# A 5-layer fp32 transformer on one core: heads' squares summed as two fp32r products, and changed orders at six places

## The chip, the cores and the metric

One core of a Trainium2 chip. The metric is the device time of one execution in microseconds (us); smaller is better. The kernel takes 1498.96 us, the median of three runs (1498.57 to 1501.03). All of the kernel is one hand-written program for the five engines: TensorE (PE, with its weight loads as PEld), VectorE (DVE), ScalarE (ACT), GpSimd (POOL) and SyncE (SP, which only issues transfers).

## The reference

For 256 positions of width 1024, in float32, four layers of one block and then one layer of another:

```python
for layer in range(4):                       # mixers: diff, stick-breaking, sliding window, diff
    h = rmsnorm(x, attn_norm[layer]); m = mixer(h)
    x = x + m @ w_o[layer]
    h = rmsnorm(x, ffn_norm[layer]); x = x + conv_gated_ffn(h)      # 2752 wide, causal conv of 3
x = rmsnorm(x, final_norm)
h = rms_norm(x, g_mix_pre); y = concat(pool_mixer, moba_attention)(h) @ w_out
x = x + rms_norm(y, g_mix_post)
h = rms_norm(x, g_ffn_pre); x = x + rms_norm(conv_ffn(h), g_ffn_post)
x = x + (p @ w_ple) * sigmoid(x @ w_ple_gate)
```

In the differential mixer (layers 0 and 3) each of the 8 heads has an output `o` of 128 columns per position, which is normalised by itself: `rmsnorm(o, subln) * (1 - lambda_init)`. That needs the sum of the squares over the head's 128 columns.

## The kernel before

**Numbers.** Everything is float32. A product runs as three fp32r matmuls: every operand is split into a high part (a cast to fp32r) and a low part (the rest), and hi x hi, lo x hi and hi x lo are summed in PSUM. A plain fp32 matmul is recorded as two matmuls of one line (the "x2" of the rows). Plain fp32 is used for the small things: scores, transposes, probabilities x values, and sums over partitions by a matmul with a matrix of ones (statistics).

**Weights.** They come as 245 chunks of 128x2048, in the order in which TensorE uses them. SP fetches a chunk into one of three raw buffers; ACT writes its high part `w_hi` (L394); DVE writes its low part `w_lo` (L919, raw minus high); TensorE uses both. SP's fetch of the third chunk after it waits for DVE's low part, which frees the raw buffer. How far ahead of use a chunk is split is written out by hand: `ahead(c, lead)` and `split_to(c)` stand at chosen places of ACT's and DVE's programs.

**Order.** Each engine's program is one fixed queue over the list STAGES (mixer projections and heads, `wo`, `up`, `down`, per layer); semaphores join them. An instruction that waits holds up everything behind it on its engine.

**Normalisation.** TensorE starts a stage before the row statistic is known: the first chunk or chunks (`raw_chunks`) use x times the gain ("raw" tiles `h_hi`, `h_lo`), and their outputs are scaled afterwards (`scaled_first`, and L1444 for `up`). Behind them `normalise` (DVE) writes hf, ACT casts it to `h_hi` (`split_h`, L444), DVE writes the even low tiles (L961) and POOL the odd ones (`low_odd`, L1544). The statistic itself is a matmul in the middle of the first chunk (`statistic`, called in `first_outputs`).

**Differential heads.** Heads go in pairs, 4 groups per layer, 16 heads in the two layers. For a head TensorE multiplies probabilities by values (`heads`, L1916 and L1917). ACT copies the result (`head_squares`, L483) and squares it (L485). TensorE sums the squares over the partitions (`head_statistic`, L1968: plain fp32 ones x squares). ACT takes the logarithm and the exponential (`head_rms`, L490 and L493), DVE scales the head (L1078), ACT and DVE split it (L499, L1083), and it is an operand of `wo`. Between these TensorE runs other work (`beside`): the projections of the next group, or, in the last group, the first parts of `wo`. An even head's statistic stands ahead of the transposes of the next head (L1905), and behind them in the last group; an odd head's stands after the next scores or next to the last `wo` parts. DVE splits chunks between its other duties (`ahead`), one of them right after the divide of the odd head, which is where the even head's squares are made. POOL, in these layers, issues the bias tables' transfers (`bias_dma`, L1539, two for each head, in a loop) and nothing else after the layer's first low tiles.

**Other places the change touches.** Layer 0's start (`first_layer`); the last group of the stick-breaking heads (`mask` on POOL, L1626, between ACT's exponential and TensorE's `heads`); the eight sliding-window head pairs (`copy_probT` L472, `exps` L464, `mix_high` L478 on ACT; `divide`, `mix_low` L1072 on DVE; TensorE's `heads` wait for both); the first two chunks of `up` and the fifth, which waits for its low part; the start of layer 4 (`mix`), where the statistic of `down3` stands after the third tile; the residual and second normalisation of layer 4 (`add_normed` L1058, L1067); and the last `add_normed` ahead of the gate.

## Time and profile before

| what | value |
|---|---|
| median of the runs | 1498.96 us (1498.57 to 1501.03) |
| the profiled execution's own time | 1498.88 us |
| its span, first to last instruction | 1497.2 us |
| granted TensorE clock, mean | 0.999 of full speed |
| busy: PE / PEld | 1487.0 us (99%) / 1423.4 us (95%) |
| busy: DVE / ACT / POOL | 1063.5 us (71%) / 879.2 us (59%) / 336.2 us (22%) |
| from memory | 262 MB, 176 GB/s over the span |
| chain that ended last, by engine | PE 87%, DVE 8%, ACT 3%, issue 1% |

The table is to be read so: where TensorE is busy nearly all the time, an instruction taken from it shortens the run by its place in the queue, and idle time of another engine is worth nothing in itself. What can be won otherwise is the few short stretches in which TensorE waits, and what can be lost is a new one.

### The profile page before, as it was taken

The numbers are of one execution on the slowest core, as the hardware profiler recorded it, in microseconds if no ns is written. First come the engines' busy times: TensorE is split into PE (matmuls) and PEld (weight loads), VectorE is DVE, ScalarE is ACT, GpSimd is POOL, SyncE is SP. The second block draws the span as 40 slices with busy tenths as digits, with TensorE's granted clock in tenths as the row PEclk, the third lists the DMA queues.
The fourth block names the chain that finished last, engine by engine and source line by source line (L and its number), as shares of the span: only waits on it lengthen the run. The fifth ranks groups of instructions, "written<-read, shape, count | busy, mean of one in ns | idle before, by whom it ended". The sixth has DMA issues, their size and how long they took to land.

```text
span 1497.2 us, 28533 instructions
## 1 busy us (share of the span) xinstructions
PE 1487.0 (99%) x11576; PEld 1423.4 (95%) x11576; DVE 1063.5 (71%) x1734; ACT 879.2 (59%) x1405; POOL 336.2 (22%) x482
## 2 busy tenths in 40 slices
PE   9999999999999999999999999999999999999998
PEld 8999999899999998989999899999998899999998
DVE  7778877565578775786887566688775778776545
ACT  7777655456766554575656347766563567544343
POOL 2103222211142222213222221032222371221101
PEclk9999999999999999999999999999999999999999
DMA  7643656443336554552665545446554554365450
GB/s 272 204 162 124 242 184 218 169 163 147 117 138 218 205 190 177 187 180 85 216 207 183 188 170 178 155 145 221 197 192 177 173 191 169 114 228 194 164 209 29
DMA packets 39694, 265.16 MB, mean 177 GB/s; under 512 B 5247, under 2 KB 5562, under 8 KB 8976
## 3 DMA queue, kind: packets, MB, share of 16 engines
q1 hardware_dynamic: 36432, 255.54, 48.4%
q0 software_dynamic: 2992, 7.79, 2.3%
q8 instruction: 91, 1.49, 0.4%
q14 instruction: 35, 0.29, 0.1%
q10 hardware_dynamic: 144, 0.05, 0.0%
HBM read 262.24 MB, written 1.12 MB: 176 GB/s over the span
## 4 chain that ended last, share of the span: by engine, by line
PE 87%; DVE 8%; ACT 3%; issue 1%; POOL 0%; ACTq 0%
PE bank L1681 21%; PE bank L1682 20%; PE bank L1683 20%; PE bank L1692 9%; PE bank L1691 4%; PE bank L1733 4%; DVE w_lo L919 4%; PE bank L1742 2%; ACT w_hi L394 1%; PE bank L1916 1%; DVE tmp L1454 1%; PE bank L1897 1%; PE bank L1896 1%; DVE tmp L965 1%; PE bank L1905 1%
## 5 line engine op out<-in xcount | busy, mean ns | idle before, releaser
L919 DVE TENSOR_TENSOR w_lo<-w_raw,w_hi 128x2048 fp32r<-128x2048 f32 x239 | 553.0, 2321 | 72.5 <-ACT w_hi L394 72.3
L1681 PE MATMUL bank<-h_hi,w_hi 128*128 128x256 f32 x1968 | 561.2, 285 | 0.8 <-DVE w_lo L919 0.8
L1682 PE MATMUL bank<-h_lo,w_hi 128*128 128x256 f32 x1968 | 556.8, 283 | 0.0
L1683 PE MATMUL bank<-h_hi,w_lo 128*128 128x256 f32 x1968 | 556.8, 283 | 0.0
L394 ACT CAST w_hi<-w_raw 128x2048 fp32r<-128x2048 f32 x239 | 453.0, 1905 | 85.3 <-DMA w_raw<-w_std 64.4
L1681 PEld LDWEIGHTS bank<-h_hi,w_hi 128*128 128x128 f32 x1968 | 377.3, 192 | 6.4 <-issue 4.2
L1682 PEld LDWEIGHTS bank<-h_lo,w_hi 128*128 128x128 f32 x1968 | 377.4, 192 | 0.1
L1683 PEld LDWEIGHTS bank<-h_hi,w_lo 128*128 128x128 f32 x1968 | 377.3, 192 | 0.0
L1692 PE MATMUL bank<-act_both,w_hi 128*128 128x512 f32 x672 | 239.0, 399 | 0.0
L1454 DVE SCALAR_TENSOR_TENSOR tmp<-bank,par,tmp 128x255 f32<-128x255 f32 (+1 forms) x346 | 149.1, 476 | 94.6 <-ACT tmp L854 93.5
L1691 PE MATMUL bank<-act_both,w_lo 128*128 128x256 f32 x672 | 188.9, 281 | 0.0
L854 ACT ACTIVATE tmp<-bank,par 128x256 f32<-128x256 f32 x173 | 88.8, 558 | 157.0 <-PE bank L1683 156.9
L1692 PEld LDWEIGHTS bank<-act_both,w_hi 128*128 128x128 f32 x672 | 126.4, 188 | 30.0
L1652 POOL CAST act_both<-tmp 128x256 f32 x110 | 53.7, 488 | 440.2 <-DVE tmp L1471 336.5
L1681 PE MATMUL bank<-act_both,w_hi 128*128 128x256 f32 x516 | 149.2, 289 | 0.0
L1682 PE MATMUL bank<-act_both,w_hi 128*128 128x256 f32 x516 | 145.9, 283 | 0.0
L1683 PE MATMUL bank<-act_both,w_lo 128*128 128x256 f32 x516 | 145.9, 283 | 0.0
L1691 PEld LDWEIGHTS bank<-act_both,w_lo 128*128 128x128 f32 x672 | 127.0, 189 | 0.0
L1733 PE MATMUL bank<-h_hi,w_hi 128*128 128x256 f32 x384 | 102.5, 289 | 0.0
L1681 PEld LDWEIGHTS bank<-act_both,w_hi 128*128 128x128 f32 x516 | 98.7, 191 | 3.0 <-issue 2.7
L1733 PE MATMUL bank<-h_hi,w_lo 128*128 128x256 f32 x384 | 100.3, 283 | 0.0
L1682 PEld LDWEIGHTS bank<-act_both,w_hi 128*128 128x128 f32 x516 | 98.8, 191 | 0.1
(219 smaller groups left out, 2116.2 us busy)
## 6 DMA issues: line engine op xcount, KB each, us to landing
w_raw<-w_std SPq DMA_DIRECT2D x239, 1024.0 KB, 4.8
act_both<-vec_dram POOLq DMA_DIRECT2D x56, 128.0 KB, 3.4
w_raw<-w_std SPq DMA_DIRECT2D x3, 512.0 KB, 7.8
x<-xT SPq DMA_DIRECT2D x2, 512.0 KB, 5.2
out<-x SPq DMA_DIRECT2D x3, 256.0 KB, 2.0
w_raw<-w_std SPq DMA_DIRECT2D x2, 256.0 KB, 4.8
par<-params SPq DMA_DIRECT2D x1, 446.0 KB, 6.0
cst<-consts SPq DMA_DIRECT2D x1, 256.0 KB, 8.8
```

The lines of the kernel that those rows point to most:

```text
L394: act.copy(w_hi[:, n % SLOTS, :], w_raw[:, n % RAW, :]).then_inc(hi_ready, 1)
L854: act.activation(to[:, slot, :], source, ACT.Identity, bias=col(3), scale=col(2)).then_inc(conv_init, 1)
L919: dve.tensor_tensor(w_lo[:, n % SLOTS, :], w_raw[:, n % RAW, :], w_hi[:, n % SLOTS, :].bitcast(F32), ALU.subtract).then_inc(lo_ready, 1)
L1454: return dve.scalar_tensor_tensor(to[:, slot, lag:S], source(v)[:, 0:S - lag], par[:, bass.ds(at + (4 * v + 2 - lag), 1)], to[:, slot, lag:S],
L1652: pool.tensor_copy(act_hi[:, bass.ds(j, 1), :].squeeze(1) if not isinstance(j, int) else act_hi[rows, j, :], cval[rows, slot, :]).then_inc ...
L1681: pe.matmul(dst, wh, xh, start=first, stop=False, skip_group_check=shared)
L1682: pe.matmul(dst, wh, xl, start=False, stop=False, skip_group_check=shared)
L1683: done = pe.matmul(dst, wl, xh, start=False, stop=last, skip_group_check=shared)
L1691: pe.matmul(bank[:, 0:S], wl, xh, start=start and k == 0, stop=False, skip_group_check=True)
L1692: done = pe.matmul(bank[:, :], wh, pair, start=False, stop=stop and k == len(weights) - 1, skip_group_check=True)
L1733: pe.matmul(dst, a, b, start=k == 0 and w is wh and (n == 0 or not shared), stop=False, skip_group_check=shared)
L1742: done = pe.matmul(dst, a, b, start=False, stop=k == DT - 1, skip_group_check=shared)
```

## The change

The squares of a head get a high and a low part. ACT casts the squares to fp32r (`square_hi`), POOL subtracts (`square_lo`, two operands from SBUF), and TensorE sums each with an fp32r matrix of ones, which ACT makes once per differential layer in the buffer of `tri_r`. The even head's statistic goes behind the transposes in all groups. The rest are changed orders: an earlier split of chunk 2 in layer 0; a later second split in the last stick-breaking group; ACT's and DVE's order in the sliding-window heads; the split of `up` chunk 5 ahead of the second chunk's taps, with a shorter wait on TensorE; in layer 4 a second raw chunk, and the statistic of `down3` after the sixth tile; and, for the two `add_normed`, gains multiplied by ACT while it takes the outputs, all low tiles of the second normalisation on DVE, each right behind the next tile.

The parts below stand in the order of the program: the buffers and ACT's lead in the last group, ACT (`head_squares`, the mixer stages, the sliding window, `wo` and `down` of layer 4), DVE (`normalise`, `add_normed`, the first layer, the start of `mix`, the last stick-breaking group, the sliding window, `up`), POOL (`square_low_of`, `low_odd`), and PE (`statistic`, the start of `mix`, the heads, `up`).

```diff
+        ones_r = tri_r
+        square_hi, square_lo = act_hi[:, DT + 2:DT + 4, :], act_lo[:, DT + 2:DT + 4, :]
...
-            return 3 if app == 0 else 2 if app % 2 and app < 9 else 1
+            return 3 if app == 0 else 2 if app % 2 and app < 9 or app == 8 else 1
...
                 act.activation(u_sb[:, 2 + slot, :], u_sb[:, slot, :], ACT.Square).then_inc(head_sq, 1)
+                act.wait_ge(head_sq, d_half + 1)
+                act.copy(square_hi[:, slot, :], u_sb[:, 2 + slot, :]).then_inc(square_high, 1)
...
+                    if c0 == 0:
+                        split_to(2)
                     (both_rms if prev == "down3" else rms)(SUMS[prev][2])
...
-                            if k:
-                                act.wait_ge(bank_free, RING + c0 + 1)
-                                act.wait_ge(used, c0 + k + 1)
-                                act.copy(u_sb[:, 2 * k:2 * k + 2, :].rearrange("p a b -> p (a b)"),
-                                         pj[slot_of(c0, k)][:, :]).then_inc(bank_free, 1)
                             ahead(c0 + k)
+                        act.wait_ge(bank_free, RING + c0 + 2)
...
+                        if da:
+                            act.wait_ge(consts_in, 16)
+                            act.copy(ones_r[:, :], ones).then_inc(ones_high, 1)
...
                             q, s = half + j, s_half + j
-                            copy_probT(s, j % 2, 2)
+                            if j not in (2, 6):
+                                copy_probT(s, j % 2, 2)
                             if j == 5:
                                 ahead(c0 + 6, HIGH)
+                                mix_high(q, j)
+                                copy_probT(s + 1, 0, 2)
                             if j < 6:
                                 exps(s + 2, j % 2, j + 3)
+                            if j != 5:
+                                mix_high(q, j)
                             if j in (1, 3):
                                 evac_q(c0 + 4 + j // 2, j // 2)
-                            mix_high(q, j)
+                            if j == 1:
+                                copy_probT(s + 1, 0, 2)
...
-                        done = act.copy(tmp[:, a:b, :].rearrange("p a b -> p (a b)"), source)
+                        for t in range(a, b):
+                            done = act.mul(tmp[:, t, :], source[:, (t - a) * S:(t - a + 1) * S], param("mix_post", t))
...
+                    if every:
+                        if k:
+                            low(k - 1)
...
-                    dve.scalar_tensor_tensor(tmp[:, k, :], tmp[:, k, :], param(gain, k),
-                                             factor, ALU.mult, ALU.mult).then_inc(dve_step, 1)
+                    dve.tensor_tensor(tmp[:, k, :], tmp[:, k, :], factor, ALU.mult).then_inc(dve_step, 1)
...
+                split_to(2)
                 dve.wait_ge(rstd_done, 1)
                 scaled(0, 1, 2, 3)
-                split_to(2)
...
+                        if kind == "mix":
+                            scaled_first(c0 + 1, u_sb[:, 2:4, :], (1.0, 1.0))
...
+                            mix_low(q, i * 2)
+                            if not more:
                                 ahead(c0 + n, HIGH)
-                            mix_low(q, i * 2)
...
+                            mix_low(half + j, j)
                             if j < 6:
                                 steps[0] += divide(s_half + j + 2, j % 2, True, steps[0])
-                            mix_low(half + j, j)
...
-                                if j == 0:
-                                    split_to(weights_of(layer, c) + RING)
+                                split_to(weights_of(layer, c) + RING)
...
+            def square_low_of(d_half, slot):
+
+                pool.wait_ge(square_high, d_half + 1)
+                pool.tensor_tensor(square_lo[:, slot, :], u_sb[:, 2 + slot, :],
+                                   square_hi[:, slot, :].bitcast(F32), ALU.subtract).then_inc(square_low, 1)
...
                         with pool.Fori(1, halves // 2) as i:
                             for b in range(2):
                                 bias_dma(table, i * 2 + (s_half + b), b, i * 2 + b)
+                            for b in range(2):
+                                square_low_of(i * 2 + (d_half - 2 + b), b)
+                        for b in range(2):
+                            square_low_of(d_half + halves - 2 + b, b)
...
-                    for k in range(lead):
-                        project(c0 + k, slot_of(c0, k), app, prev if k == 0 else None)
+                    if lead:
+                        project(c0, slot_of(c0, 0), app, prev, False)
+                        project(c0 + 1, slot_of(c0, 1), app, "raw")
...
+                    if da:
+                        pe.wait_ge(ones_high, layer // 3 + 1)
...
-                        pe.wait_ge(head_sq, d + 1)
-                        pe.matmul(tp[1][:, 0:S], ones, u_sb[:, 2 + slot, :], start=True, stop=True)\
+                        pe.wait_ge(square_low, d + 1)
+                        pe.matmul(tp[1][:, 0:S], ones_r[:, :], square_hi[:, slot, :], start=True, stop=False)
+                        pe.matmul(tp[1][:, 0:S], ones_r[:, :], square_lo[:, slot, :], start=False, stop=True)\
                           .then_inc(head_stat, 1)
...
-                        if da and more:
-                            head_statistic(d, 0)
                         transposes(s + 1, 1, maps)
-                        if da and not more:
+                        if da:
                             head_statistic(d, 0)
...
-                        if k == RING and layer < 4:
+                        if k in (RING, RING + 1) and layer < 4:
                             pe.wait_ge(lo_ready, weights_of(layer, c) + 1)
-                            pe.wait_ge(first_scaled, first_scaled_count(ffn, 1))
+                            pe.wait_ge(first_scaled, first_scaled_count(ffn, 2 * (k - RING) + 1))
```

## Rows read from the trace of the kernel before

**Rows 1.** The page: busy us of each engine, share of the span, instructions.

```profile
PE 1487.0 (99%) x11576; PEld 1423.4 (95%) x11576; DVE 1063.5 (71%) x1734; ACT 879.2 (59%) x1405; POOL 336.2 (22%) x482
```

**Rows 2.** Waits of PE: engine, what waits, for what: us, times, longest.

```profile
PE bank L1842 <- DVE acc L953: 1.1, 1, 1.1
PE bank L1681 <- DVE w_lo L919: 1.0, 5, 0.2
PE bank L1916 <- DVE act_both L1072: 0.9, 2, 0.5
PE bank L1742 <- DVE h_lo L961: 0.7, 2, 0.4
PE bank L1916 <- issue: 0.5, 1, 0.5
PE bank L1742 <- POOL h_lo L1544: 0.5, 1, 0.5
PE bank L1916 <- ACT tmp L472: 0.5, 3, 0.2
```

**Rows 3.** Timeline of PE at `up`: start us, us, what, xcount [idle before].

```profile
148.04 0.28 PE L1683 MATMUL bank<-h_hi,w_lo 128*128 128x256 f32 x1
148.55 0.39 PE L1681 MATMUL bank<-h_hi,w_hi 128*128 128x256 f32 x1 [0.22 <-DVE w_lo L919]
148.77 0.28 PE L1682 MATMUL bank<-h_lo,w_hi 128*128 128x256 f32 x1
148.89 0.29 PE L1683 MATMUL bank<-h_hi,w_lo 128*128 128x256 f32 x1
```

**Rows 4.** Timeline of PE, layer 0: a statistic, the last group's heads and statistic.

```profile
88.82 0.59 PE L1968 MATMUL bank<-u_sb,cst 128*128 128x256 f32 x2
89.25 0.49 PE L1905 MATMUL bank<-cst,tmp 128*128 128x128 f32 x3
...
89.70 0.28 PE L1682 MATMUL bank<-w_lo,h_hi 128*128 128x256 f32 x1
...
108.44 0.70 PE L1916 MATMUL bank<-tmp,vtok 128*128 128x256 f32 x2 [0.15 <-ACT tmp L472]
...
111.34 0.59 PE L1968 MATMUL bank<-u_sb,cst 128*128 128x256 f32 x2
```

**Rows 5.** Single lines: count, shortest/median/longest ns, first to last start us.

```profile
L1968 PE MATMUL bank<-u_sb,cst x32: 377/379/382, 44.5 to 979.7; 128*128 128x256 f32 x32
...
L444 ACT CAST h_hi<-tmp x80: 391/407/410, 28.6 to 1281.6; 128x256 fp32r<-128x256 f32 x80
...
L1559 POOL TENSOR_TENSOR h_lo<-proj,h_hi x39: 730/740/876, 121.7 to 1262.0; 128x256 fp32r<-128x256 f32 x39
```

**Rows 6.** Timeline of ACT, layer 0: squares (L485) and a logarithm (L490).

```profile
86.54 0.42 ACT L485 ACTIVATE u_sb<-u_sb 128x256 f32<-128x256 f32 x1
...
105.80 0.42 ACT L485 ACTIVATE u_sb<-u_sb 128x256 f32<-128x256 f32 x1
...
108.32 0.48 ACT L490 ACTIVATE u_sb<-bank,odd 128x256 f32<-128x256 f32 x1
...
110.51 0.42 ACT L485 ACTIVATE u_sb<-u_sb 128x256 f32<-128x256 f32 x1
```

**Rows 7.** Timeline of POOL in layer 0's `up`.

```profile
138.53 2.79 POOL L1544 TENSOR_TENSOR h_lo<-tmp,h_hi 128x256 fp32r<-128x256 f32 x1
```

**Rows 8.** Timeline of DVE: the low parts of five weight chunks.

```profile
43.10 2.28 DVE L919 TENSOR_TENSOR w_lo<-w_raw,w_hi 128x2048 fp32r<-128x2048 f32 x1
...
86.62 2.29 DVE L919 TENSOR_TENSOR w_lo<-w_raw,w_hi 128x2048 fp32r<-128x2048 f32 x1
...
106.60 2.28 DVE L919 TENSOR_TENSOR w_lo<-w_raw,w_hi 128x2048 fp32r<-128x2048 f32 x1
...
110.58 2.28 DVE L919 TENSOR_TENSOR w_lo<-w_raw,w_hi 128x2048 fp32r<-128x2048 f32 x1
...
137.85 2.86 DVE L919 TENSOR_TENSOR w_lo<-w_raw,w_hi 128x2048 fp32r<-128x2048 f32 x1
```

More of the change, by code:

```diff
@@ L225, in build @@
         head_sq = sem("head_sq")
+        ones_high = sem("ones_high")
+        square_high = sem("square_high")
+        square_low = sem("square_low")
         head_stat = sem("head_stat")
@@ L880, in _ @@
                             squares(name, k, pj[slot_of(c0, k)][:, 0:S])
-                            act.copy(tmp[:, k, :], pj[slot_of(c0, k)][:, 0:S]).then_inc(bank_free, 1)
+                            act.mul(tmp[:, k, :], pj[slot_of(c0, k)][:, 0:S], param("ffn_post", k))\
+                               .then_inc(bank_free, 1)
                             if k == 2:
@@ L953, in add_squares, with normalise @@
                         dve.tensor_tensor(total, a, b, ALU.add).then_inc(acc_done, 1)
-            def normalise(app, norm, behind=None):
+            def normalise(app, norm, behind=None, every=False):
                 dve.wait_ge(rstd_done, norm + 1)
@@ L966, in normalise @@
                                              ALU.mult, ALU.mult).then_inc(hf_done, 1)
-                    if k % 2 and k > 1 and behind is None:
+                    if every:
+                        if k:
+                            low(k - 1)
+                    elif k % 2 and k > 1 and behind is None:
                         low(k - 3)
+                if every:
+                    low(DT - 1)
+                    return
                 if behind is not None:
@@ L1053, in divide, with add_normed @@
                 return done
-            def add_normed(gain, factor, signal, after):
+            def add_normed(factor, signal, after):
                 def scaled(k):
-                    dve.scalar_tensor_tensor(tmp[:, k, :], tmp[:, k, :], param(gain, k),
-                                             factor, ALU.mult, ALU.mult).then_inc(dve_step, 1)
+                    dve.tensor_tensor(tmp[:, k, :], tmp[:, k, :], factor, ALU.mult).then_inc(dve_step, 1)
                     steps[0] += 1
@@ L1395, in _ @@
                         dve.wait_ge(rstd_done, SUMS[name][2] + 1)
-                        add_normed("mix_post", mix_rstd, x_ready, sum_behind)
+                        add_normed(mix_rstd, x_ready, sum_behind)
                         ahead(c0 + 2, AHEAD)
-                        normalise(app, SUMS["res_a"][2])
+                        normalise(app, SUMS["res_a"][2], every=True)
                         ahead(c0 + 1, AHEAD)
@@ L1510, in low @@
                                                   ALU.subtract).then_inc(h_lo_even, 1)
-                        add_normed("ffn_post", rstd[:, :], hf_done, low)
+                        add_normed(rstd[:, :], hf_done, low)
                         split_to(CHUNKS)
@@ L1639, in _ @@
                     raw_low(app)
-                    low_odd(app, hf)
+                    if layer < 4:
+                        low_odd(app, hf)
                     app += 1
@@ L1750, in first_outputs @@
                             statistic("x")
-                    elif raw not in (None, "x", "raw") and k == {"d": 2, "w": 4}.get(raw[0], 5):
+                    elif raw not in (None, "x", "raw") and k == (5 if raw == "down3" else {"d": 2, "w": 4}.get(raw[0], 5)):
                         statistic(raw)
```

13 lines of the change are left out of this document (7 added, 6 removed).

## The prediction

> **What bounds the kernel.** I read the page's busy times first: PE is busy for 1487.0 us, 99% of its span, DVE for 71%, ACT for 59%, POOL for 22% [rows 1]. So only two things count: what PE itself executes, and the short stretches in which it waits. The second view is the list of PE's waits; the change aims at seven of its lines, which hold 5.2 us of idle time together [rows 2]. The third is PE's timeline around one such wait: at 148.04 the last product of a chunk starts, the next at 148.55 after 0.22 us of idle time and the one after at 148.77. That is 0.73 us for what takes 0.24 in a row without a break (two steps of 0.12, as from 148.77 to 148.89) [rows 3]. So a wait ahead of an fp32r product costs its idle time and about 0.27 us of emptying and refilling on top. Then come PE's rows at two statistics of the heads [rows 4], the single lines' durations [rows 5], and what ACT, POOL and DVE do at the same moments [rows 6 to 8], since the new subtraction runs on POOL while DVE splits weights.
>
> The terms are summed against the profiled execution's own time, 1498.88 us, with its span of 1497.2 in it; the median of the runs is 0.08 us above that, so the two are the same here. A measurement of this kernel can tell about 0.2% from no change, 3.0 us: "same" is 1496.0 to 1502.0.
>
> **Part 1, the heads' statistics, on PE.** The plain statistic takes from 88.82 to 89.25 [rows 4], 0.43 us; two fp32r products take 2 x 0.12 = 0.24 [rows 3]. Saved: 0.19 us for each of 16 heads, 3.0 us if nothing waits.
>
> **Part 1, the new chain.** Behind the squares stands a cast on ACT (0.41 us by L444, same shape [rows 5], 0.44 with its start), then a subtraction on POOL, both inputs from SBUF. Its nearest undisturbed row is L1559, 0.74 us [rows 5]. But one of its inputs there comes from PSUM. With both from SBUF, one that started at 138.53, inside DVE's low part of a chunk (137.85 to 140.71), took 2.79 us and ended at 141.32, 0.61 behind it [rows 7, 8]. DVE's low part has two SBUF inputs too and takes 2.28 us [rows 8]. So I bound a subtraction by 0.74 us on one side and "end of the low part plus 0.61" on the other, and take the second wherever a low part covers its start, since that row has its operands.
>
> The Trainium skill ("SBUF — State Buffer", section "SBUF: two separate sides") says that VectorE with two SBUF inputs and a GpSimd operation that reads SBUF exclude each other for the whole instruction. By that rule alone the subtraction would take its full 0.74 us behind the low part instead of 0.61: ten stalls x 0.13, which would make the sum 1501.3 instead of 1500.0.
>
> *Ordinary even heads (5).* The squares start at 86.54 [rows 6]; the cast ends near 87.4, inside the low part of 86.62 to 88.91 [rows 8]. The subtraction is ready at 88.91 + 0.61 = 89.52. PE arrives behind the transposes, 89.25 to 89.70 with a pipeline that overlaps by 0.12 [rows 4]: 88.82 + 0.33 = 89.15. Stall 0.37, less 0.19 saved: +0.18 each, +0.9 in all.
> *First even head.* Low part from 43.10, statistic at 44.5 [rows 5, 8]: ready at 45.38 + 0.61 = 45.99, arrival 44.83, stall 1.1: +0.9.
> *Ordinary odd heads (6).* No low part lies over their chain and they have over 1 us to spare: -0.19 each, -1.1.
> *Even head of the last group (2).* Squares end at 106.22 [rows 6], the cast at 106.66, just inside the low part of 106.60 to 108.88 [rows 8]. Ready at 109.49, the sums end at 109.73, and the next head's product starts at 109.83 instead of 108.44 [rows 4]: +1.4 each, +2.8.
> *Odd head of the last group (2).* The even head's late statistic moves its logarithm from 108.32 [rows 6] to about 110.0, and with DVE's scaling behind that the next low part from 110.58 to 112.28 [rows 8]. It ends at 114.56. The squares, at 110.51 [rows 6], come 1.4 later, so their cast ends at 112.8, inside it; ready at 115.17. PE arrives at 111.34 [rows 4] + 1.4 = 112.74: stall 2.43, with 0.1 of restart and 0.19 saved +2.35 each, +4.7.
> Part 1 together: 0.9 + 0.9 - 1.1 + 2.8 + 4.7 = **+8.2 us**.
>
> **Part 1, what it puts beside other work.** ACT gets 16 casts and two copies of the ones, under 8 us on an engine that is 59% busy [rows 1]; where its copy for the next head is already what PE waits for (0.15 us [rows 4]), a cast of 0.44 ahead of it could show, but there the subtraction is later still and hides it. With that gone it would cost up to 0.44 a group. POOL's two bias transfers of a group now stand behind its subtractions, so they go out up to 3 us later; the table is wanted a group later (the even heads of two neighbouring groups lie 20 us apart, 88.82 and 108.44 [rows 4]). No other queue is passed.
>
> **Part 2, the six changed orders.** *`up`, the fifth chunk's low part:* PE waits for it 5 times, 1.0 us, 4 in `up`, one at the start [rows 2]; with 0.27 of restart each 2.3 us. It goes because the low part now stands ahead of the second chunk's taps. Late next are these taps, by up to 1.8 us; PE no longer waits for both of them at once, only for the chunk's own, and POOL's split behind may be held by the low part as above. Between 0 and 2.3 gained, or worse (a rival). I take 2.3. SP's fetch behind each low part moves with it, by at most 4 us, against buffers two chunks ahead.
> *The start of layer 0:* chunk 2's low part 3 us earlier, with the transfer behind it; small stalls, 0.15 us, and at worst one new wait of the same size.
> *Layer 4's start:* the statistic of `down3` waits 1.1 us for DVE's sum (L1842) [rows 2]; three tiles later and with a second raw chunk, it goes with its restart: 1.3. ACT's and DVE's scaling of the second raw chunk adds 0.7 us of DVE, beside PE's next chunk.
> *Second normalisation:* PE waits twice for DVE's low tiles (L961), 0.7 [rows 2]. POOL's low tiles go, and so does what they hold back; each tile is then a product and a low part on DVE. 0.7 + 0.54 = 1.25, at worst 0, if DVE's pace per tile is just PE's.
> *The last `add_normed`:* 0.5 <- POOL h_lo [rows 2] with 0.27, of which I take half, 0.4.
> *Last stick-breaking group:* 0.5 before L1916, which the list calls issue [rows 2]; 0.55.
> *Sliding window:* 0.9 <- act_both and the part of 0.5 <- ACT tmp that isn't the two last groups' 0.15 [rows 2, 4], 0.2: 1.1.
> Sum: 2.3 + 0.15 + 1.3 + 1.25 + 0.4 + 0.55 + 1.1 = **-7.1 us**. For layer 4's `wo`, where multiplications take the place of copies on ACT, I add nothing: they hide beside the raw chunks' products on PE; without that cover they would cost up to 0.75 us.
>
> **Net:** +8.2 - 7.1 = +1.1. 1498.9 + 1.1 = **1500.0 us**, no change that can be measured. Its own range, with each bound of part 2 and 0.3 us either way on the last group's four stalls, is 1497 to 1503.
>
> **Rivals.**
> *A. POOL is not held.* L1559's 0.74 us speak for it [rows 5], the row at 138.53 against it [rows 7]. Then every ordinary head gains 0.19, 12 x 0.19 = 2.3; the last even heads lose some 0.4 by ACT's cast ahead of the copy; the last odd ones, squares ended at 110.93 [rows 6], are ready at 110.93 + 0.44 (shift) + 0.44 + 0.15 + 0.74 = 112.7 against 111.8: +0.8 each. Part 1 is +0.1, the time 1498.9 - 7.1 + 0.1 = 1491.9 us. Chance 0.15.
> *B. The wait at `up` comes back one chunk later.* The taps stand behind a low part of 2.28 us, or 2.86 where POOL is in its way [rows 8], and the chunk after next waits for its own. I put their slack at 0.7 to 0.9 us, an estimate. It decides where they come more than that late: then the 1.8 gained in the four `up` is gone and 4 x 1.3 of new wait (0.9 to 1.0 of lateness, 0.27 restart) comes: 1500.0 + 1.8 + 5.2 less what overlaps, 1504.5 us, slower. For it speaks that DVE's split and POOL's exclude each other [rows 7]; against it that the wait now is only 0.2 us long at its longest [rows 2]. Chance 0.12.
> *C. It doesn't do what it says:* the restarts don't come back with the idle time, and part 2 brings 5.2 of idle at most, or half of it, 2.6 to 5.2: 1502 to 1504 us. Chance 0.05.
> The main case has 0.68.
>
> **How the numbers follow.** The predicted time is the main case's, 1500.0. Its range of 1497 to 1503 holds about 0.8 of its 0.68; to leave out no more than 2 in 10 in all, the range goes down towards A, to 1493, and up to B's 1504.5. Faster by over 0.2%: all of A, 0.15, and 0.06 of the main case. Slower: all of B, most of C, and 0.14 of the main case, where its two largest terms, the last groups' stalls, run over: 0.30. Same: the rest, 0.49.
>
> **What would show it right or wrong.** In the changed profile PE's waits should list the statistic's line <- POOL square_lo: some 10 entries, about 0.37 us five times, 1.1 once, and the longest in the last groups, 1 to 2.4 us. Each of the late subtractions should last 1 to 2.5 us and end 0.6 behind a w_lo; if they all last 0.74, A is right. L1842, w_lo, act_both, h_lo and L1916's issue should be gone from the waits. A new wait of `up` on u_sb or act would show B. If PE's busy time doesn't fall by about 3 us, the two products don't take 0.24. The forecast fails if the subtraction's wait sits in another place than the last groups, or if what frees PE there is not POOL but ACT.

## The result, and the profile after

The changed kernel takes 1515.4 us (median; 1514.97 to 1515.95, 4 runs) where the kernel before took 1499.06 in the same session: a ratio of 1.0108, 95% interval 1.0096 to 1.012. That is 16.3 us slower, where 1500.0 was forecast with a range of 1493 to 1504.5. The profiled execution spans 1514.1 us, 16.9 more than before.

The page of the changed kernel, busy us of each engine (beside [rows 1]):

```profile
PE 1489.3 (98%) x11576; PEld 1426.6 (94%) x11576; DVE 1063.6 (70%) x1740; ACT 887.5 (59%) x1425; POOL 373.8 (25%) x494
```

and TensorE's waits in it (what waits, for what: us, times, longest; beside [rows 2]):

```profile
PE bank L2006 <- POOL act_both L1603: 9.7, 10, 2.4
PE bank L1716 <- ACT tri_r L602: 3.7, 1, 3.7
PE bank L1931 <- DVE small L1023: 2.2, 1, 2.2
PE bank L1777 <- POOL h_lo L1567: 1.9, 1, 1.9
PE bank L1716 <- ACT vtok L519: 1.5, 1, 1.5
...
PE bank L1931 <- ACT proj L738: 0.6, 1, 0.6
PE bank L1951 <- DVE act_both L1093: 0.2, 1, 0.2
```

Five of the seven old lines are gone, as forecast (L1842 <- acc, w_lo, DVE's h_lo, the issue entry, ACT's L472), act_both has shrunk to 0.2, and the statistic (now L2006) waits for POOL's subtraction (L1603) ten times. But four lines are new and a fifth has grown, none of them forecast: for the ones in fp32r (L602), for scores and token copies in layer 4 (L1023, L519), for POOL's low tile in the last stage (L1567, 1.9 where it was 0.5), and for ACT's copy in the sliding window (L738).

PE's busy time rose by 2.3 us where a fall of about 3 was to show that two products take 0.24. They do: where nothing waits, the statistic's two products and the next one start 0.12 apart (96.25, 96.36 and 96.48 us in e9). Busy time also grows where the clock is low, which four of these waits brought with them (below): in e4, with the same products and one such stretch, it is 1484.3.

How far the changed kernel's TensorE lies behind the one before at the same product tells where the time went. The steps of that distance (us, + is later) are these:

| place | forecast | measured |
|---|---|---|
| layer 0, up to 27 us | -0.6 | -1.1 |
| layer 0, wait for the ones | 0 | +5.2 |
| statistics, 12 ordinary heads | +0.7 | +0.8 |
| last groups, even heads (2) | +2.8 | +2.7 |
| last groups, odd heads (2) | +4.7 | +6.3 |
| `up`, 4 times | -1.8 | -1.8 |
| last stick-breaking group | -0.55 | -0.6 |
| sliding window | -1.1 | -0.6 |
| statistic of `down3` | -1.3 | -1.4 |
| layer 4's heads | 0 | +5.5 |
| second normalisation | -1.25 | -1.0 |
| last stage | -0.4 | +2.85 |
| sum | +1.1 | +16.9 |

Three rows hold 14 of the 15.8 us by which the forecast was short, and two of them were forecast as nothing.

**The ones.** TensorE in the changed kernel, layer 0, then ACT (start us, us, what [idle before]):

```profile
29.62 0.28 PE L1718 MATMUL bank<-w_hi,h_lo 128*128 128x256 f32 x1
33.62 0.58 PE L1716 MATMUL bank<-h_hi,w_hi 128*128 128x256 f32 x1 [3.72 <-ACT tri_r L602]
34.00 0.41 PE L1717 MATMUL bank<-h_lo,w_hi 128*128 128x256 f32 x1
34.21 0.41 PE L1718 MATMUL bank<-h_hi,w_lo 128*128 128x256 f32 x1
```

```profile
33.03 0.21 ACT L587 ACTIVATE root_gain<-root_gain 128x8 f32<-128x8 f32 x1
33.27 0.30 ACT L602 CAST tri_r<-cst 128x128 fp32r<-128x128 f32 x1
```

The copy of the ones costs ACT 0.30 us, but it stands in ACT's queue behind the first head's exponentials, which wait for scores, and TensorE waits for it ahead of the first group of heads, although the ones are first used at 49.4 us. The trace of the kernel before showed it: there the instruction ahead of the new copy ends at 34.3 us, and TensorE passes the place of the new wait at 30.8.

```profile
34.11 0.21 ACT L578 ACTIVATE root_gain<-root_gain 128x8 f32<-128x8 f32 x1
```

**The heads.** POOL's subtractions and DVE's low parts of chunks in the changed kernel, layer 0 (beside [rows 7, 8]):

```profile
91.90 2.02 POOL L1603 TENSOR_TENSOR act_both<-u_sb,act_both 128x256 fp32r<-128x256 f32 x1 [5.26 <-ACT act_both L492]
99.70 0.75 POOL L1603 TENSOR_TENSOR act_both<-u_sb,act_both 128x256 fp32r<-128x256 f32 x1 [5.78 <-ACT act_both L492]
111.30 2.74 POOL L1603 TENSOR_TENSOR act_both<-u_sb,act_both 128x256 fp32r<-128x256 f32 x1 [10.85 <-ACT act_both L492]
117.75 2.01 POOL L1603 TENSOR_TENSOR act_both<-u_sb,act_both 128x256 fp32r<-128x256 f32 x1 [3.71 <-ACT act_both L492]
```

```profile
91.04 2.29 DVE L935 TENSOR_TENSOR w_lo<-w_raw,w_hi 128x2048 fp32r<-128x2048 f32 x1
...
111.17 2.29 DVE L935 TENSOR_TENSOR w_lo<-w_raw,w_hi 128x2048 fp32r<-128x2048 f32 x1
116.89 2.29 DVE L935 TENSOR_TENSOR w_lo<-w_raw,w_hi 128x2048 fp32r<-128x2048 f32 x1
```

The subtraction outside a low part takes 0.75 us; the three inside one end 0.58 to 0.59 behind it (91.90 + 2.02 = 93.92 against 93.33; 114.04 against 113.46; 119.76 against 119.18). The forecast had 0.61.

The row of the 12 ordinary heads agrees with its forecast partly by luck. The first even head was to stall for 1.1 us and cost 0.9; TensorE came late to it, behind the wait for the ones, and it cost 0.33. The other five even heads cost 0.32 each instead of 0.18: the idle time was shorter than forecast (0.25 at 93.98 us, for 0.37), but the emptying and refilling behind it, about 0.27 us, had been left out of their sum. The six odd ones gained 0.18 each, as forecast.

**The clock.** The same stall cost 2.5 us in layer 0 and 3.8 in layer 3. Here are two products behind it in each, and the windows over them (length; busy us and count of PE, PEld, DVE, ACT and POOL; the last three numbers are the granted clock, the share of the DMA engines and GB/s). The third window lies behind the wait for POOL's low tile in the last stage:

```profile
119.81 0.39 PE L2006 MATMUL bank<-act_both,tri_r 128*128 128x256 f32 x1 [2.41 <-POOL act_both L1603]
120.03 0.28 PE L2007 MATMUL bank<-act_both,tri_r 128*128 128x256 f32 x1
...
989.69 0.58 PE L2006 MATMUL bank<-act_both,tri_r 128*128 128x256 f32 x1 [2.42 <-POOL act_both L1603]
990.07 0.41 PE L2007 MATMUL bank<-act_both,tri_r 128*128 128x256 f32 x1
```

```profile
120.00:121.50 1.50, 1.50 (x14) 1.50 (x14) 0.19 (x1) 0.89 (x2) 0.00 (x0) 1.00 0.89 191
...
990.00:992.60 2.60, 2.60 (x13) 2.60 (x13) 0.65 (x2) 1.30 (x3) 0.00 (x0) 0.50 0.99 312
...
1487.00:1491.50 4.50, 4.50 (x26) 4.50 (x27) 3.09 (x3) 4.48 (x3) 2.12 (x3) 0.62 0.00 0
```

After 2.41 us of idling the granted clock stayed at 1.00 in one place; after 2.42 us it was 0.50 (the lower level, 1.2 GHz) for 2.6 us in the other, twelve products came every 0.213 us instead of 0.12, and that cost 12 x 0.093 = 1.1 us more. Behind the wait for the ones it was thirteen products, 1.2 us: 3.72 us of idle time, 0.42 of emptying and refilling and this 1.2 come to 5.35, and 0.2 of it the kernel before loses at the same products too, which leaves 5.2. In the last stage fifteen products came so, 1.4 us, and in layer 4 ten. The Trainium skill ("TensorE: Matmul & The Clock Gate", Part 1) says that a gate sets TensorE's clock by how busy it has been recently, and that the number of products at the lower clock varies from run to run. The traces agree: each stretch at 0.50 here follows a wait of 1.5 to 3.7 us, and behind the same wait of 3.72 us for the ones it was 13 products in this run and 21 in e5.

**Layer 4.** DVE at the scores of the second head pair, and some of POOL's pooling windows ahead of it, in the changed kernel:

```profile
1244.68 0.06 DVE L1016 MEMSET wait_mark<- 128x1 f32 x1 [6.97 <-DMA act_both<-vec_dram]
```

```profile
1204.78 2.26 POOL L1633 TENSOR_TENSOR sq<-sq,par 128x16 f32<-128x16 f32 x1
1207.01 2.84 POOL L1634 TENSOR_SCALAR sq<-sq 128x240 f32<-128x240 f32 x1
...
1214.50 2.14 POOL L1633 TENSOR_TENSOR sq<-sq,par 128x16 f32<-128x16 f32 x1
1216.61 2.84 POOL L1634 TENSOR_SCALAR sq<-sq 128x240 f32<-128x240 f32 x1
...
1239.88 2.21 POOL L1562 DMA_DIRECT2D act_both<-vec_dram  x4 [0.30 <-POOL act_both L1638]
```

The same transfers in the kernel before:

```profile
1224.04 2.20 POOL L1539 DMA_DIRECT2D act_both<-vec_dram  x4 [0.30 <-POOL act_both L1609]
```

The pooling windows are a chain of small operations on POOL from 1203.94 to 1239.6, 35.6 us; before it ran from 1193.51 to 1223.7, 30.2 us. L1633 takes 0.22 us when nothing is in the way and 2.14 to 2.35 where it meets a low part. Seven operations of the chain last over 2 us so, four did before. Behind the chain stand the transfers of the next table. In the kernel before they left at 1224.04; TensorE is 9.6 us later here, so they leave 6.3 us later against its work (5.4 by the chain, 0.9 by its start); DVE waits 7 us for them, and TensorE waits for DVE's scores (2.2) and ACT's copies behind these (1.5).

**The last stage.** POOL's first low tile, and DVE meanwhile, in the changed kernel:

```profile
1482.10 4.75 POOL L1567 TENSOR_TENSOR h_lo<-x,h_hi 128x256 fp32r<-128x256 f32 x1 [60.25 <-ACT h_hi L909]
```

```profile
1482.15 0.42 DVE L1088 TENSOR_TENSOR x<-x,tmp 128x256 f32<-128x256 f32 x1
1482.49 0.42 DVE L1080 TENSOR_TENSOR tmp<-tmp,rstd 128x256 f32<-128x256 f32 x1
...
1485.51 0.75 DVE L1088 TENSOR_TENSOR x<-x,tmp 128x256 f32<-128x256 f32 x2
```

POOL was held through twelve DVE operations in a row and ended 0.59 behind the last of them (1486.85 against 1486.26), where DVE paused for the first time. Of the 2.85 us, 1.4 are the longer wait (1.9 for 0.5) and 1.4 the lower clock behind it. In the kernel before the same tile took 1.14 us, and the DVE operation that it met 0.96 instead of 0.48. There DVE's scaling was a scalar_tensor_tensor that read its gain from SBUF (`par`):

```profile
1468.22 1.14 POOL L1544 TENSOR_TENSOR h_lo<-x,h_hi 128x256 fp32r<-128x256 f32 x1 [60.43 <-ACT h_hi L893]
```

```profile
1468.68 0.96 DVE L1058 SCALAR_TENSOR_TENSOR tmp<-tmp,par,rstd 128x256 f32<-128x256 f32 x1
```

### The profile page after: what moved, and what is told of

It reads as the page before. It is cut to its first block, busy times and chain, and to the rows that moved or that the text cites. A ratio compares the mean times of both kernels' runs of the same rounds, so it can differ in the third digit from the quotient of the medians.

```text
span 1514.1 us, 28578 instructions
## 1 busy us (share of the span) xinstructions
PE 1489.3 (98%) x11576; PEld 1426.6 (94%) x11576; DVE 1063.6 (70%) x1740; ACT 887.5 (59%) x1425; POOL 373.8 (25%) x494
## 4 chain that ended last, share of the span: by engine, by line
PE 87%; POOL 4%; DVE 3%; ACT 3%; issue 2%; DMA 0%; POOLq 0%; ACTq 0%; DVEq 0%
PE bank L1716 19%; PE bank L1717 19%; PE bank L1718 19%; PE bank L1727 10%; PE bank L1768 6%; PE bank L1726 5%; PE bank L1777 3%; POOL act_both L1603 1%; ACT tmp L469 1%; PE bank L1951 1%; DVE tmp L1023 1%; PE bank L2301 0%; POOL sq L1634 0%; POOL sq L1633 0%; DVE w_lo L935 0%
```

## The experiments

The kernel before was timed in each session beside them: 1499.35 us with e1 to e4, 1498.75 with e5 to e8, 1499.39 with e9 to e11. Unless an edit says otherwise, it is made on the changed kernel.

**e1: the heads' part undone.**

```diff
-                act.copy(square_hi[:, slot, :], u_sb[:, 2 + slot, :]).then_inc(square_high, 1)
...
-                        pe.wait_ge(square_low, d + 1)
-                        pe.matmul(tp[1][:, 0:S], ones_r[:, :], square_hi[:, slot, :], start=True, stop=False)
-                        pe.matmul(tp[1][:, 0:S], ones_r[:, :], square_lo[:, slot, :], start=False, stop=True)\
+                        pe.wait_ge(head_sq, d + 1)
+                        pe.matmul(tp[1][:, 0:S], ones, u_sb[:, 2 + slot, :], start=True, stop=True)\
```

> The changed kernel with the heads' part undone (plain fp32 sum of the squares, no cast, no subtraction, no ones in fp32r, even statistic back ahead of the transposes), the six changed orders kept. My theory: the heads' part costs 5.3 us by TensorE's wait for the ones in layer 0, 3.8 and 5.1 us in the two last groups and 0.8 us in the ordinary groups, 15.0 us together, so about 1500.4 us. Rival, by the forecast on record: the heads' part costs 8.2 us, so 1507.2 us, and the six orders cost the rest. Second rival: the waits only stand for others that take their place, and less than 5 us come back, above 1510 us.

Measured: 1501.45 us (1500.8 to 1506.09, 10 runs), ratio 1.0018, interval 1.0008 to 1.0028. The heads' part costs 13.9 us, not 8.2, and the six orders together, forecast at 7.1 us faster, make the kernel 2 us slower. The profiled execution was one of the longer ones (1505.2): DVE waited 2.5 us in layer 0 for the first bias transfer, and TensorE 2.5 for DVE. Without that wait and what comes with it (3.9 us) the two profiled executions are 14.4 us apart.

**e2: the wait for the ones ahead of the first statistic.**

```diff
-                    if da:
-                        pe.wait_ge(ones_high, layer // 3 + 1)
...
+                        pe.wait_ge(ones_high, layer // 3 + 1)
                         pe.wait_ge(square_low, d + 1)
```

> The changed kernel with one edit: TensorE waits for the fp32r ones only ahead of the first statistic, not ahead of the first group of heads. My theory: the 3.7 us wait at 29.6 us goes with its restart and the lower granted clock behind it, 5.3 us in all, so 1510.1 us, and nothing takes its place. Rival: ACT's queue is late there for its other work too, and the next product that needs ACT (its token copies, or the split of the next chunk) waits in its stead: at least 1513.5 us.

Measured: 1511.52 us, ratio 1.0084 (1.0067 to 1.0101). The 3.7 us wait is gone and no other stands in its place; at 37 us TensorE is 5.2 us ahead of the changed kernel. 0.8 of that is given back at the first even head, whose subtraction TensorE now reaches early enough to wait for, 1.09 us where the forecast had 1.1:

```profile
45.18 0.36 PE L2005 MATMUL bank<-act_both,tri_r 128*128 128x256 f32 x1 [1.09 <-POOL act_both L1603]
```

The wait for the ones had hidden that stall.

**e3 and e5: how DVE multiplies in the last stage.**

```diff
-                    dve.tensor_tensor(tmp[:, k, :], tmp[:, k, :], factor, ALU.mult).then_inc(dve_step, 1)
+                    dve.scalar_tensor_tensor(tmp[:, k, :], tmp[:, k, :], 1.0,
+                                             factor, ALU.mult, ALU.mult).then_inc(dve_step, 1)
```

> The changed kernel with one edit: in the two add_normed DVE multiplies by a scalar_tensor_tensor with the number 1.0 in place of a tensor_tensor (same operands, same result). My theory: POOL's first low tile of the last stage, which took 4.75 us, is held by an unbroken row of tensor_tensor operations and gets its turn where a scalar_tensor_tensor stands in the row, as in the kernel before; it lasts about 1.1 us again and the wait of 1.9 us for it shrinks to 0.5 or less: 1512.3 to 1513.0 us. Rival: only the tightness of DVE's row counts (no pause between its operations), not the kind of operation, and nothing changes: 1515.4 us, the POOL operation above 4 us again.

Measured: 1517.43 us (1514.94 to 1520.07), ratio 1.012 (1.01 to 1.014). The POOL operation lasts 4.75 us again: my theory fell as I had put it, since the kind of operation alone changes nothing. Its profiled execution (1517.8) is 2.1 us longer than the changed kernel's for another reason: DVE waited 1.9 us for the first bias transfer in layer 0, and TensorE 5.8 instead of 3.7 for the ones. In e5 the 1.0 is `ones[:, 0:1]`, a column in SBUF.

> The changed kernel with one edit: in the two add_normed DVE multiplies by a scalar_tensor_tensor whose scalar is read from a column of ones in SBUF (as the kernel before read its gain), where the run with the number 1.0 in the instruction left POOL's 4.75 us as it was. Theory: what lets POOL in is that DVE must read this scalar from SBUF before it takes its two tiles; POOL's first low tile of the last stage lasts about 1.1 us again, the wait for it falls from 1.9 to at most 0.5 us, and the last stage is 2.5 to 2.9 us shorter. Rival: POOL got in before only because ACT was later or DVE's row had a pause somewhere; then the POOL operation lasts above 4 us again.

Measured: 1514.47 us (2 runs), ratio 1.0092 (1.0062 to 1.0123), and, what tells, POOL and DVE in e5:

```profile
1483.81 1.14 POOL L1568 TENSOR_TENSOR h_lo<-x,h_hi 128x256 fp32r<-128x256 f32 x1 [60.43 <-ACT h_hi L909]
```

```profile
1483.93 0.42 DVE L1089 TENSOR_TENSOR x<-x,tmp 128x256 f32<-128x256 f32 x1
1484.26 0.96 DVE L1080 SCALAR_TENSOR_TENSOR tmp<-tmp,cst,rstd 128x256 f32<-128x256 f32 x1
```

1.14 instead of 4.75 us, and now it is DVE's operation that is held (0.96 instead of 0.48): POOL took its turn just where DVE had a scalar to read from SBUF. TensorE's wait for that tile is gone, and the last stage is 3.0 us shorter than the changed kernel's. The whole run gained only 0.9 us, in two runs, and 1.5 in the profiled execution. There 21 and 14 products behind two earlier waits came at the lower clock, where the changed kernel's profile has 13 and 12 behind its two, and five more in layer 4: 1.4 us.

**e4: the transfers ahead of the fourth pooling window.**

```diff
                         for g, w in enumerate(WINDOWS):
+                            if g == 3:
+                                for h in range(2, halves):
+                                    bias_dma(table, s_half + h, h % 2, h)
```

> The changed kernel with one edit: in layer 4 POOL issues the bias transfers of the second head pair ahead of the fourth pooling window, not behind it. My theory: DVE's wait of 7.0 us for that transfer, and with it TensorE's waits of 2.2 and 1.5 us and the low clock behind them, go: 5.5 us less, 1509.9 us. Rival: the fourth window, now 2.2 us later, is what TensorE waits for instead (its product for the pooled tiles stands at 1242.95 us, and POOL ended at 1239.6): a new wait of up to 1.5 us, 1511 to 1512 us. Second rival: the stall belongs to the second raw chunk itself and not to the transfer: no change, 1515.4 us.

Measured: 1512.24 us, ratio 1.0089 (1.0072 to 1.0106). Of TensorE's waits in e4 this one is new:

```profile
PE bank L1719 <- POOL act_both L1641: 1.5, 1, 1.5
```

The waits for scores and token copies are gone, and over layer 4's heads TensorE gains 3.7 us on the changed kernel: the transfer was the cause. The first rival is right about the rest: the fourth window now ends 4.6 us later, 2.1 by the four issues ahead of it and the rest because three of its operations now last 2.1 to 2.7 us, where two lasted 2.2 and 2.4.

**e10: the start of layer 4 put back.** One raw chunk, the statistic behind the third tile, ACT copying the second chunk's outputs.

```diff
-                    elif raw not in (None, "x", "raw") and k == (5 if raw == "down3" else {"d": 2, "w": 4}.get(raw[0], 5)):
+                    elif raw not in (None, "x", "raw") and k == {"d": 2, "w": 4}.get(raw[0], 5):
...
-                        project(c0 + 1, slot_of(c0, 1), app, "raw")
...
-                            scaled_first(c0 + 1, u_sb[:, 2:4, :], (1.0, 1.0))
```

> The changed kernel with the start of layer 4 put back as before: one raw chunk, the statistic behind the third tile, ACT copying the second chunk's outputs. Theory: the 5.5 us lost behind the late transfer come from this edit alone (POOL's windows start later against DVE's chunk splits and are held more often); it goes, and the gain of 1.3 us at the statistic is lost: 1515.4 - 5.5 + 1.3 = 1511.2 us. Rival: the windows were delayed by what came before (the lateness of the whole run changes nothing), or by ACT's and DVE's other moved orders; then the wait for the transfer stays and the time is 1515 us or more.

Measured: 1511.98 us, ratio 1.0077 (1.0061 to 1.0092). The waits for L1023 and L519 are gone and the old one is back:

```profile
PE bank L1879 <- DVE acc L973: 1.1, 1, 1.1
```

In the profiled execution TensorE loses 1.4 us on the changed kernel at the statistic and gains 5.5 over layer 4's heads. Four operations of POOL's windows last over 2 us, as in the kernel before, and the chain takes 30.2 us again. So the edit that won 1.4 us at the statistic lost 5.5 us 50 us later, with no other edit needed. (That execution was the longest of the four, 1516.6: DVE waited 1.9 us for the first bias transfer in layer 0, and TensorE 5.8 for the ones.)

**e6: without the low part.** No subtraction, one fp32r product, which waits for ACT's cast.

```diff
-                        pe.wait_ge(square_low, d + 1)
-                        pe.matmul(tp[1][:, 0:S], ones_r[:, :], square_hi[:, slot, :], start=True, stop=False)
-                        pe.matmul(tp[1][:, 0:S], ones_r[:, :], square_lo[:, slot, :], start=False, stop=True)\
+                        pe.wait_ge(square_high, d + 1)
+                        pe.matmul(tp[1][:, 0:S], ones_r[:, :], square_hi[:, slot, :], start=True, stop=True)\
```

> The changed kernel without the low parts of the squares: no subtraction on POOL, and one fp32r product (high part) for the statistic, which waits for ACT's cast. It leaves out the low part of the sum. My theory: all of the heads' cost behind the ones is POOL's leg; 9.7 us of waits, restarts and low clock go, 16 x 0.31 = 5.0 us of products are saved against plain fp32, and the cast itself costs about 0.4 us in each of the last groups' heads, 1.2 us: 1515.4 - 9.7 - 3.8 = 1501.9 us. Rival: ACT's cast, ahead of the copy that the next head needs, is itself late; then the waits stay with ACT as what they wait for, 1506 us or more.

Measured: 1502.8 us (1500.41 to 1504.72, 10 runs), ratio 1.002 (1.0007 to 1.0033). What is left of the heads in its list of waits, beside the one for the ones (4.5):

```profile
PE bank L1947 <- ACT tmp L477: 1.8, 2, 0.9
```

All ten waits at the statistic were POOL's leg. The cast has a price of its own only in the last groups, where TensorE waits 0.9 us for ACT's copy for the odd head instead of the 0.15 of the kernel before [rows 4].

**e7: the chunks' low parts moved behind the heads' low tiles in the last group.**

```diff
-                            elif da:
-                                ahead(c0 + n)
...
                                 if not more:
-                                    ahead(c0 + n, HIGH)
+                                    ahead(c0 + n)
...
                                 head_low(q + 1, 1, t + 1)
+                                if not more:
+                                    ahead(c0 + n, HIGH)
```

> The changed kernel with one edit: in the last group of a differential layer DVE writes the low part of each of the two chunks behind the head's low tile, not ahead of its scaling, so that no two-input DVE operation runs while POOL subtracts. My theory: the subtractions there last 0.74 us, the waits of 1.7 and 2.4 us go with restarts and the low clock behind them, 8.3 of 8.9 us: 1507.1 us. Rival: the chunks' low parts are then late and TensorE waits for w_lo in their place, so that at most 4 us come back: above 1511 us. Second rival: POOL was not held by DVE but slow by itself: its operations stay above 2 us and nothing changes.

Measured: 1515.22 us, ratio 1.0099 (1.0074 to 1.0123): no gain in the whole, though neither rival holds as put. POOL and DVE's low part in e7, layer 0, last group, and TensorE's waits:

```profile
112.69 0.75 POOL L1603 TENSOR_TENSOR act_both<-u_sb,act_both 128x256 fp32r<-128x256 f32 x1 [10.83 <-ACT act_both L492]
117.81 2.00 POOL L1603 TENSOR_TENSOR act_both<-u_sb,act_both 128x256 fp32r<-128x256 f32 x1 [4.37 <-ACT act_both L492]
```

```profile
116.94 2.29 DVE L935 TENSOR_TENSOR w_lo<-w_raw,w_hi 128x2048 fp32r<-128x2048 f32 x1
```

```profile
PE bank L2006 <- POOL act_both L1603: 5.4, 8, 2.0
...
PE bank L1951 <- ACT tmp L477: 1.6, 2, 0.8
```

The even head's subtraction, free of the low part, takes 0.75 us and its wait is gone, which shows the lock once more from the other side. But the next limit, ACT's copy, is only 0.9 us behind (0.8 of wait), and the low part now stands where the odd head's subtraction is: 2.0 us of wait instead of 2.4. I had looked at where each low part was taken away, not at where it came to lie. In its two places the edit does gain, 2.5 us in the profiled execution; 1.2 are lost at the wait for the ones, ahead of the edit, where 22 products instead of 13 came at the lower clock, and 0.4 in layer 4. All four executions have a mean granted clock of 0.993 or 0.994, those of the changed kernel 0.995. Whether the edit or chance moved these stretches isn't shown.

**e8: the six orders, two of them mended.** e1 with the last `add_normed` as before (gain in DVE's operation, copies on ACT) and the third head's transfers alone ahead of the fourth window.

```diff
+                            if g == 3:
+                                bias_dma(table, s_half + 2, 0, 2)
...
-                        add_normed(rstd[:, :], hf_done, low)
+                        add_normed(rstd[:, :], hf_done, low, "ffn_post")
```

> The kernel of e1 (six changed orders, heads as before) with two things mended: the last add_normed as in the kernel before (gain in DVE's operation, copies on ACT), and in layer 4 the transfers of the third head's table ahead of the fourth pooling window. e1 took 1501.45 us. By the traces the last stage gives back 2.9 us, and the layer-4 wait of 5.5 us falls to 0.4 with 0.3 of restart: 1493.8 us, 5.5 us faster than the kernel before. Rival: each mend uncovers a wait of the same size behind it (DVE's scaling of the second raw chunk, the pooled tiles): 1497 us or more.

Measured: 1493.11 us (1492.7 to 1494.95, 6 runs), ratio 0.9953 (0.9935 to 0.9972): faster than both kernels, and as expected within 0.7 us.

**e11: the changed kernel with both mends and e2's.** It differs from e8 by the heads' part alone.

> The changed kernel with all heads split as it has them and three mends: TensorE waits for the ones ahead of the first statistic, the last add_normed as before, and the third head's transfers ahead of the fourth window. It differs from e8 by the heads' part alone. Theory: the heads' part costs 9.7 us by its POOL leg, so 1493.1 + 9.7 = 1502.8 us, slower than the kernel before by 3.6 us. Rival by the forecast on record: 8.2 us, 1501.3 us. Rival: the waits interact and the heads' part costs less than 5 us once the others are gone: below 1498 us.

Measured: 1504.72 us (1502.42 to 1506.73, 8 runs), ratio 1.0031 (1.002 to 1.0042). The heads' part costs 11.6 us, more than my 9.7. The two were timed in different sessions; their profiled executions are 12.9 us apart, and 1.6 of that is no part of the heads: TensorE waited 1.5 us in layer 0 for DVE, and DVE for the first bias transfer. In the other 11.3 the first even head's stall is back in view (1.1, e2), and one of the last groups' waits met the low clock (13 products, 1.2):

```profile
PE bank L2010 <- POOL act_both L1606: 11.2, 10, 2.5
```

**e9: e8 with the split squares in six heads.** Only the odd heads outside the last groups, whose subtraction nobody waited for; all others plain, in their old places.

```diff
+                        if slot and d % 8 < 7:
+                            pe.wait_ge(ones_high, layer // 3 + 1)
+                            pe.wait_ge(square_low, d // 8 * 3 + d % 8 // 2 + 1)
```

> The kernel of e8 with the squares split and summed as two fp32r products in the six odd heads alone that are not in a layer's last group (their subtraction took 0.75 us and nobody waited for it); all others plain fp32 in their old places, and the wait for the ones ahead of the first of these statistics. Theory: each saves 0.19 us, 1.1 us together: 1492.0 us against the 1493.1 of e8. Rival: the cast on ACT ahead of its copies for the next group makes a new wait in each group, as large as the gain: 1493 us or more.

Measured: 1492.21 us (1492.01 to 1492.65, 5 runs), ratio 0.9948 (0.9934 to 0.9961). The busy times of e9 and what is left of its waits:

```profile
PE 1484.0 (100%) x11576; PEld 1422.0 (95%) x11576; DVE 1064.7 (71%) x1740; ACT 882.4 (59%) x1415; POOL 348.5 (23%) x484
```

```profile
PE bank L1979 <- DVE rstd L1113: 1.4, 1, 1.4
PE bank L1934 <- ACT proj L739: 0.6, 1, 0.6
PE bank L1719 <- DVE act_both L1259: 0.4, 1, 0.4
```

0.9 us below e8, where 1.1 was expected. These two also were timed in different sessions, and their medians alone would not settle so small a difference; the traces do. TensorE's distance to e8 falls by 0.17 to 0.18 us at each of the six heads (0.64 us at 16 us, 0.47, 0.29, 0.11 in layer 0, then -0.07, -0.25, -0.43 in layer 3) and moves nowhere else: 1.07 us. This is the best of the versions.

## Why the prediction was wrong

**What held.** The mechanism of the heads: ten waits of some 10 us in all (9.7 measured), each late subtraction 0.6 us behind a low part, 0.75 where none is in the way, the waits in the last groups 1.7 and 2.4 us. Rival A (POOL not held) is refuted by these rows. The rule of the Trainium skill ("SBUF — State Buffer", "SBUF: two separate sides"), worked out as the full 0.74 behind the low part, was not what POOL did: 0.59, close to the 0.61 of [rows 7, 8]. That the ordinary heads' sum came out (0.8 for 0.7) is partly luck, as said at the table. Of part 2, the gains at `up`, the statistic of `down3`, the stick-breaking group and the second normalisation came within 0.25 us of their terms. Rival B (the wait at `up` comes back one chunk later) didn't happen: w_lo and the taps are in no line of waits. Rival C (the restarts don't come back) didn't either: each `up` gave back 0.45 us for 0.2 of idle time.

**Step that failed, 1: the ones (+5.2).** "ACT gets 16 casts and two copies of the ones, under 8 us on an engine that is 59% busy" prices an instruction by its duration. The term was put at nothing, and its price was in its place: a new wait on TensorE for an instruction at the end of a queue that was itself late. I had worked out for the subtraction who waits for it, and for the copy not. e2 took the wait away and nothing came in its place.

**Step 2: layer 4's start (+5.5).** The sum took the 1.3 us at the statistic and named DVE's extra 0.7 us as hidden "beside PE's next chunk". Who waits for what DVE makes there was not followed: POOL's windows start from these outputs, they are a chain of 30 us with several DVE low parts across it, and the next table's transfers stand behind it. I had told of POOL's queue for the heads, and not for the stage in which POOL is busiest. e4 and e10 show transfer and edit as the cause, and with the old start four of POOL's operations are held again instead of seven. Which part of the moved start does it (the second raw chunk, DVE's scaling of it, the later statistic) was not tried by itself.

**Step 3: the last stage (+2.85 for -0.4).** Priced as if DVE's new operation, 0.42 instead of 0.48 us, were only shorter. The instruction it replaced was what let POOL in. No row of the kernel before shows an unbroken run of such operations beside a POOL operation, so this could not be read there; but a bound from both sides would have had "held until DVE's run ends" as its bad end. e3 and e5 show it. Half of the loss, 1.4 us, is the lower clock behind the wait, which no term of the sum held.

**Step 4: the last odd heads (+6.3 for +4.7), sized too small.** The stall was as forecast (2.41 for 2.43), but restart was taken as 0.1 to 0.27 for any length. After a stall of that size the granted clock was 0.50 for 2.6 us in one of two places, 1.1 us more. The same is missing at the waits of steps 1, 2 and 3: 13, 10 and 15 products at the lower clock, 3.5 us together.

**Step 5: sliding window (-0.6 for -1.1).** The two waits on act_both fell to 0.2 in all, but ACT's copies of the next projections, now behind `mix_high`, make a new one of 0.6 (L738). I had not said what is late next there, as I had for `up`.

## What to carry to other kernels

The cost of a new instruction on an engine with room is not its duration but the latest thing it stands behind and the first thing that stands behind it; follow both ends, on POOL's and DMA's queues too, and 50 us further on. Where DVE read two SBUF inputs, a POOL subtraction of two SBUF tiles that began beside it ended some 0.6 us behind it, or behind a whole unbroken run of such operations. Save on the engine that bounds only where the new chain has slack, head by head: the same replacement was worth 0.18 us in six places and cost up to 3.8 in the others.

## What the runs showed of the hardware

- POOL was held 4.75 us by twelve DVE tensor_tensor operations in a row; a scalar_tensor_tensor with an immediate number didn't help (4.75), one that reads its scalar from SBUF did (1.14). By the Trainium skill ("SBUF — State Buffer", "SBUF: two separate sides") whichever starts first holds the shared ports for the whole instruction, which would have let POOL in behind one operation of 0.42 us; the measurement decides. What in the engine makes the difference isn't shown.
- Waits of the same length (2.41 and 2.42 us) left the granted clock at 1.00 or at 0.50. Such a dip cost 0.9 to 1.4 us here. Part of the spread between executions goes with it: in e4 the fastest (1510.1) has a mean granted clock of 0.999, the two slowest (1513.4 and 1513.6) 0.997.
- The first bias transfer of layer 0 (128 KB) lands unnoticed in seven of the thirteen profiled executions and holds DVE for 0.6 to 2.5 us in the other six (e1 2.5, e3 1.9, e4 0.6, e6 0.6, e10 1.9, e11 1.6). That is as large as some of the effects above; what sets it isn't shown.
